# Recurrent stage: dense products moved from the solve to a place behind the transitions

## What is computed

```
def step(s, inp):
    r_t, w_t, k_t, v_t, kk_t, a_t = inp
    sa = einsum('bhij,bhj->bhi', s, -kk_t)
    s = (s * w_t[:, :, None, :] + sa[..., None] * (kk_t * a_t)[:, :, None, :]
         + v_t[..., None] * k_t[:, :, None, :])
    return s, einsum('bhij,bhj->bhi', s, r_t)
```

## Time and profile before

| | us |
|---|---|
| median of three runs | 3861.1 |
| lowest and highest | 3860.64 and 3867.76 |
| the profiled execution | 3860.53 |
| its span, first to last instruction | 3858.8 |

### The profile page before, as it was taken

How to read it: one execution, slowest core, us unless ns; L and a number is a source line. 1 busy time by engine, 2 the same in 40 slices (tenths; PEclk the granted TensorE clock), 3 DMA queues, 4 the chain that set the end, 5 groups by cost and what they waited for, 6 DMA issues and landing times. The chain is left out here.

```text
span 3858.8 us, 66595 instructions
## 1 busy us (share of the span) xinstructions
PE 3641.5 (94%) x29287; PEld 3094.6 (80%) x29287; DVE 2228.0 (58%) x4273; ACT 537.3 (14%) x991; POOL 82.8 (2%) x86
## 2 busy tenths in 40 slices
PE   6999999989989899999999899999989899999999
PEld 4466666667767899999999467667767899999999
DVE  4265555555334788889866545555552666654644
ACT  2222122222100100000000312322221100000000
POOL 0000000000000000000000000000000000000000
PEclk8989999999999999999999999999999999999999
DMA  9622333333348587787667254534413566664553
GB/s 342 209 73 76 86 96 93 88 86 105 87 158 275 181 259 240 243 262 230 191 219 241 93 176 149 162 115 152 153 66 129 161 202 203 202 196 156 167 164 126
DMA packets 680354, 637.94 MB, mean 165 GB/s; under 512 B 42093, under 2 KB 670338, under 8 KB 678658
## 3 DMA queue, kind: packets, MB, share of 16 engines
q1 hardware_dynamic: 569120, 558.96, 45.6%
q10 hardware_dynamic: 110946, 74.73, 6.7%
HBM read 627.36 MB, written 6.29 MB: 164 GB/s over the span
## 5 line engine op out<-in xcount | busy, mean ns | idle before, releaser
L1828 PE MATMUL bank<-extra,work 128*128 128x128 f32 x4224 | 478.9, 275 | 0.0
L1828 PEld LDWEIGHTS bank<-extra,work 128*128 128x128 f32 x4224 | 475.2, 192 | 0.0
L623 DVE SCALAR_TENSOR_TENSOR work<-weight_ring,silu_c,work 128x256 f32<-128x256 f32 x1050 | 421.0, 476 | 0.0
L1828 PE MATMUL bank<-work,weight_ring 128*128 128x128 f32 x2816 | 328.0, 278 | 30.5 <-PEq L717 30.5
L1828 PEld LDWEIGHTS bank<-work,weight_ring 128*128 128x128 f32 x2816 | 322.0, 194 | 31.2 <-issue 31.2
L1972 DVE TENSOR_TENSOR work<-weight_ring 128x2048 f32<-128x2048 f32 (+1 forms) x76 | 129.3, 1701 | 304.4 <-DMA weight_ring<-in_w_gate_up 169.2
L965 PE MATMUL bank<-work,x_channels 128*128 128x256 f32 (+1 forms) x736 | 247.7, 476 | 4.4 <-ACT work L1335 3.9
L1884 PE MATMUL bank<-work,weight_ring 128*128 128x128 f32 x2112 | 247.2, 275 | 0.0
L1884 PEld LDWEIGHTS bank<-work,weight_ring 128*128 128x128 f32 x2112 | 241.7, 192 | 3.3 <-issue 3.3
L2352 PE MATMUL bank<-work,weight_ring 128*128 128x512 f32 x448 | 205.5, 604 | 2.1 <-PEq L2141 2.1
L965 PEld LDWEIGHTS bank<-work,x_channels 128*128 128x128 f32 x736 | 137.2, 199 | 73.7 <-issue 52.3
(11 more groups left out here) (400 smaller groups left out, 5294.0 us busy)
## 6 DMA issues: line engine op xcount, KB each, us to landing
weight_ring<-in_w_mod SPq DMA_DIRECT2D x80, 2048.0 KB, 9.6
weight_ring<-in_w_gate_up SPq DMA_DIRECT2D x44, 2048.0 KB, 9.5
weight_ring<-in_w_in SPq DMA_DIRECT2D x26, 2048.0 KB, 9.9
weight_ring<-in_w_down SPq DMA_DIRECT2D x32, 1536.0 KB, 6.9
weight_ring<-in_w_gate SPq DMA_DIRECT2D x22, 2048.0 KB, 8.2
weight_ring<-in_w_up SPq DMA_DIRECT2D x22, 2048.0 KB, 11.8
weight_ring<-in_w_down SPq DMA_DIRECT2D x32, 1280.0 KB, 6.1
weight_ring<-in_w_out SPq DMA_DIRECT2D x16, 2048.0 KB, 9.2
```

The lines of the kernel that those rows point to most:

```text
L623: ins = v_.scalar_tensor_tensor(a, w[:, k, :], c, a, ALU.mult, ALU.add)
L1828: last = mm(out[:, m * P:(m + 1) * P], left[p][:, k, m * P:(m + 1) * P], right[p][:, k, :], start=k == 0, stop=k == 7)
```

## The change

The budget of the fill in `solve` falls from 12.0 to 9.0, and a new fill of 3.0 is called between `transitions(hp, 1)` and `read_rows(hp)`. It sets no mark.

```diff
@@ -785,7 +785,7 @@
 MOD_GROUP = 2
-FILL = {"first": 3.0, "value": 7.0, "ahead": 6.0, "solve": 12.0, "gram": 2.5, "between": 3.0, "chain": 1.5, "step": 0.95}
+FILL = {"first": 3.0, "value": 7.0, "ahead": 6.0, "solve": 9.0, "gram": 2.5, "between": 3.0, "rows": 3.0, "chain": 1.5, "step": 0.95}
 WBUFS = 4
@@ -1255,6 +1255,7 @@
                 transitions(hp, 0)
                 fill(FILL["between"])
                 transitions(hp, 1)
+                fill(FILL["rows"])
                 read_rows(hp)
                 fill(FILL["chain"], (hp, 0))
                 for n in range(1, 15):
```

## The result

| | before | changed |
|---|---|---|
| median us (lowest to highest) | 3862.0 (3860.6 to 3867.8) | 3813.9 (3809.9 to 3817.1) |
| ratio, 95% interval | | 0.9872 [0.9855, 0.9889] |
| a second session, median us | 3863.3 | 3809.2, ratio 0.9868 [0.9851, 0.9884] |
| the profiled execution, span | 3860.5, 3858.8 | 3817.1, 3815.3 |

The change takes 48 us off in one session and 54 in the other; 53 were forecast. With a fourth run of the kernel before, its median is 3862.0 and not the 3861.1 that the forecast started from. One execution of an experiment, sync_late, took 6223.7 us at a mean granted clock of 0.555 and is left out of its time.

The account below looks back on a forecast made before the run. TensorE is busy 94% of the span, so only its idle and half-clock time can be won. Terms 1 and 2 (17.9), 3 (20.6) and 4 (14.5) sum to 53.0 us, from 3861.1 to 3808; range 3799 to 3836.

Parts of the forecast that it names:

- Term 1: Row products: TensorE's 2.84 us wait for VectorE's last transitions copy goes in eight rounds, a gain of 22.7 us.
- Term 2: Solve: with 3.52 us of dense work moved out, TensorE waits for VectorE's additions, a cost of 4.8 us.
- Term 3: Second halves of transitions: instruction-refill pauses shrink as three weight loads move behind them, a gain of 20.6 us.
- Term 4: Rounds 1 to 7: the granted clock stays up from solve to chain instead of halving, a gain of 14.5 us.
- Rival (b): Transitions' pauses shrink, but the clock still dips because short idle times remain; 3823 us, 17 in 100.
- (a): Only the row products' wait goes; transitions' pauses are no refills or stay as long, clock stays low; 3843 us, 12 in 100.
- (c): Solve turns VectorE-bound: all 3.52 us lost in seven rounds, 24.6 instead of 4.8; 3828 us, 6 in 100.
- (d): Slower: the three loads land late and the cg product of chain step 7 waits; 3885 us, 2 in 100.
- (e): The new fill ahead of the row products finds no dense work and nothing changes; 3861 us, 1 in 100.

Follow-up runs that it names:

- sync_late: Changed kernel with SyncE's four small loads for the next round held until that round's row products are done; 3808.5 us, ratio 0.9858.
- from_chain: Changed kernel with the new fill's 3.0 taken from the chain's steps (0.95 to 0.72), solve back at 12.0; 3834.6 us, ratio 0.9933.
- three_places: Changed kernel with the solve at 10.0 and the fill ahead of the first transitions half cut from 2.5 to 1.5; 3811.4 us, ratio 0.9863.
- late_loads: Kernel before with ScalarE's three weight loads issued after the row products, no dense product moved; 3841.7 us, ratio 0.9948.
- light_after: Changed kernel with dense weight loads after the first four cut to one block of 128 rows (64 KB); 3809.6 us.
- pad32: Changed kernel with 8 tiny products (32 instructions) added at the start of the stage's PE program; 3808.6 us, ratio 0.9859.
- pad64: Changed kernel with 16 tiny products (64 instructions) added at the start of the stage's PE program; 3813.9 us, ratio 0.9878.
- between6: Changed kernel without the new fill, its budget given to the fill between the transitions' halves (6.0), solve kept at 9.0; 3850.8 us, ratio 0.997.

## Why the prediction came out right, and where its terms did not

The time lies in the range, 6 us above the forecast in one session and 1 us above it in the other. That it is so near is in part luck: the profiled execution gained 43.5 us where 53.0 were forecast, and terms 3 and 4 were each some 4 to 5 us too large. By terms, against the profiled execution: inside the stage it is 44.4 us shorter, and the terms find 42.7 of them. The other 1.7 lie in round 7's solve, where the clock is low for 3.4 us instead of 6.8. Outside the stage, where the change does nothing, 2.0 us were gained ahead of round 1's first solve product and 2.9 lost behind the stage, which leaves the 43.5.

**Term 1, forecast 22.7, measured 22.7.** Shown by the waits list and, taken alone, by from_chain, which has no wait at L1195 either.

**Term 2, forecast -4.8, measured about -6.** From the solve's first product to the first half of the transitions, rounds 2 to 6 shortened by 2.72 us each where 3.52 had moved, so 0.80 were lost against 0.72 forecast; round 1 lost 1.7 instead of 1.17, and round 8 0.4 where none was forecast. The mechanism is shown twice: by the new line L1163 <- L1617, and by three_places, where it goes.

**Term 3, forecast 20.6, measured 15.8.** The loads' part was right: the five halves fell from 38.45 us, and late_loads shows the cause. The step that failed is "the next packet ends after the 3.5 us of dense work that now stands between, so their second half takes 2.55". The five halves came to 21.9 and not 19.2, and round 2's grew by 1.75, while 1.4 came back at L1195 as forecast; the first halves took 0.4 more in all, and rounds 7 and 8 cancel (1.0 more and 1.0 less). I had taken the refill to be asked for when a packet ends. The runs say some 70 to 80 instructions later: with 37, 51 and 65 quick instructions left ahead of the dense work, the packet starts only 3.9 to 4.0 us after that work does, behind its end, so the work delays the refill instead of hiding it. Before the change 68 instructions stood in that place, and the packet started 0.4 to 1.1 us after the first of them. So moving the mod job out left rounds 2, 4 and 6 with second halves 1.6 to 1.75 us over the 2.55 of the forecast.

That the pauses are refills was inferred in the forecast; the traces show it. In the fourteen traces the transitions have 151 pauses of over 0.7 us, and each one ends 1.2 to 1.7 us behind the end of an instruction packet. The packet itself takes 0.9 to 1.6 us in all of them. In the 124 pauses of up to 2.6 us it starts before the pause or at most 0.2 us into it; in the 26 of 3.4 us and more it starts 0.9 to 3.3 us into it (and in the one between, of 3.0 us, 0.5). A long pause is a packet that starts late, not one that is slow. The longest of before, round 6 (852.73 to 857.77 us): up to 855.1 the engines carry data alone (queue: packets, MB, share of 16 engines' time), then the instruction packet starts.

```profile
q10 hardware_dynamic: 1078, 0.54, 91.2%
q1 hardware_dynamic: 339, 0.15, 27.8%
...
q8 instruction: 1, 0.02, 256.9%
```

**Term 4, forecast 14.5, measured 10.3.** The part that was read off the rows came out (it gives round 1 as 4.2 us in one sentence and 4.4 in the next, which changes nothing): from the row products to the local products (L1204) rounds 1 to 7 gained 14.5 us beside the 1.4 of the pause, and the row products fell from 1.98 to 1.09. Round 8 added 2.9 that I had given up. The step that failed is "a pause of 2 us alone leaves the clock up", taken from round 4 of before: in this execution the granted clock fell behind the pauses of rounds 1, 3, 7 and 8, and as the new place is filled, it is filled at the low level: 7.1 us back in all (0.5 of them in round 6, at the full clock). Rival (b) was thus a part of the truth, in some rounds of each execution.

**The rivals.** (a) falls by late_loads, and with it what the rule of the Trainium skill's page "Runtime: NRT & Kernel Launch", section "Instruction fetch mechanics", would have made of the time. The trace agrees with its blocks of 256 (the pauses lie 255 or 510 instructions apart, the packets are of 16 KiB) and not with a store of 2048 instructions and crossings that are mostly hidden: a second pause came 255 instructions behind the first, and its packet started only after the first was over. (c) came true for 6 of 24.6 us. (d) is excluded by the time, and light_after, with small loads, is no faster. (e) is excluded by the stretch of 2.83 us in the new place.

**What stays open.** Why small loads leave longer pauses than absent ones. When a refill is asked for: the traces show when its packet starts, not the request, so that it queues behind the loads is argued, not shown. What sets the 3.9 us between the start of the dense work and the packet. And why a pause of 2 us brings the clock down in one round and not in another.

## What to carry to other kernels

When a wait is covered with work from elsewhere, ask what else travels with that work: here the end of two jobs sets off three weight loads, and where they land was worth about as much as the wait (15.8 beside 22.7 us). Idle time of TensorE that comes shortly before dense work has a second price, the clock at which that work runs; read the granted clock behind each wait, not only the wait. And the long runs of very small instructions here (384 in 2.55 us) wait for their own supply: count them against the packets of the instruction queue, see when each packet starts, and put the cover behind that point.

## What the runs showed of the hardware that was not expected

- TensorE's instruction pauses move with the instruction count: 32, 64 or 128 tiny instructions at the start of the stage moved every pause of the eight rounds.
- They are refills: each of 151 pauses ends 1.2 to 1.7 us behind the end of a 16 KiB instruction packet.
- The next packet is asked for late: with 69 instructions ahead of the dense work it started 4.3 us after that work did, with 83 ahead 0.4 us after (pad32; with 101 in pad64 also 0.4).
- A pause of about 2 us beside a DMA share of 0.3 or less becomes 3.5 to 5 us in the kernel before with a share of 1.1, and there the packet starts late. between6 has short ones at the same share, where the packet started 0.8 to 1.3 us after the engines had filled.
- The same program has its granted clock fall behind a 2 us pause in some rounds and not in others, and in other rounds the next time: 16 us of round 4, around the same pause, have 1.00 in one execution of the changed kernel and 0.89 in the next.

```profile
602.00:618.00 16.00, 12.86 (x415) 7.82 (x417) 7.96 (x20) 0.24 (x1) 4.95 (x4) 1.00 0.17 32
...
600.00:616.00 16.00, 14.12 (x415) 8.22 (x417) 7.79 (x19) 0.17 (x1) 4.94 (x4) 0.89 0.18 32
```
